# Second attention: GpSimd scales the exponentials, TensorE turns them with transposes, and two weight splits move into the loop of units

## The reference

```
s_loc = einsum(q, k_window) * scale + bias        # 384 columns in the kernel, masked with -1e30
s_ctx = einsum(q, k_ctx) * scale                  # 256 columns
p = softmax(concat([s_loc, s_ctx]), axis=-1)
o = einsum(p_loc, v_window) + einsum(p_ctx, v_ctx)
o = o * silu(c_z)                                 # later in the block
```

## Time and profile before

| | |
|---|---|
| median of 3 runs | 2630.74 us (2629.36 to 2631.32) |
| span of the profiled execution, first to last instruction | 2631.7 us |
| TensorE busy | 2435.6 us (93%) |
| VectorE busy | 1163.6 us (44%) |
| ScalarE busy | 854.4 us (32%) |
| GpSimd busy | 764.2 us (29%) |
| mean granted TensorE clock | 0.965 of full |
| second attention, first units to last | 1431 us to 1820 us of the span |

### The profile page before, as it was taken

The page is one execution under the profiler, slowest core; times in us unless marked ns, Lnnn a source line. Parts: engine busy times, 40 slices in busy tenths (PEclk is TensorE's granted clock), DMA queues, the critical chain, the costliest instruction groups (busy, mean ns, idle before and its releaser), DMA issues.

```text
span 2631.7 us, 32586 instructions
## 1 busy us (share of the span) xinstructions
PE 2435.6 (93%) x12094; PEld 2045.6 (78%) x12094; DVE 1163.6 (44%) x1376; ACT 854.4 (32%) x1137; POOL 764.2 (29%) x667
## 2 busy tenths in 40 slices
PE   2797999887999999999978989889999999999997
PEld 2686888776888888888767888879778888888885
DVE  7766888685442344234453351625221121222234
ACT  3225777314221122124444343434112111112221
POOL 3343222241333333333312111020223333333331
PEclk8897999998999999999988999999999999999998
DMA  5310000550111111111121101101001111111131
GB/s 222 137 66 34 25 16 25 216 208 32 48 48 48 48 48 48 48 58 50 38 95 59 61 27 50 52 16 62 32 28 48 48 48 52 48 48 40 48 120 72
DMA packets 45708, 165.49 MB, mean 63 GB/s; under 512 B 4048, under 2 KB 5840, under 8 KB 44496
## 3 DMA queue, kind: packets, MB, share of 16 engines
q1 hardware_dynamic: 45648, 164.67, 17.7%
HBM read 156.26 MB, written 8.39 MB: 63 GB/s over the span
## 4 chain that ended last, share of the span: by engine, by line
PE 83%; DVE 9%; ACT 4%; issue 2%; DMA 1%; POOL 0%; DVEq 0%; SPq 0%; ACTq 0%; POOLq 0%
PE acc L597 63%; PE bank L833 3%; PE turn L820 3%; PE turn L698 2%; PE bank L712 2%; DVE ADA L1290 2%; PE acc L681 2%; PE bank L698 1%; PE acc L806 1%; PE bank L588 1%; DVE K2L L1629 1%; DMA XT<-in_xT 1%; PE turn L615 1%; PE bank L876 1%; DVE K2L L1630 1%
## 5 line engine op out<-in xcount | busy, mean ns | idle before, releaser
L597 PE MATMUL acc<-HH,WH 128*128 128x512 f32 x1888 | 592.1, 395 | 50.5 <-POOL HL L508 29.5
L597 PE MATMUL acc<-HL,WH 128*128 128x512 f32 x1888 | 585.4, 391 | 0.0
L597 PE MATMUL acc<-HH,WL 128*128 128x512 f32 x1888 | 584.7, 391 | 0.0
L495 POOL TENSOR_TENSOR WH<-WF,CON 128x16 fp32r<-128x16 f32 x186 | 53.6, 288 | 1576.8 <-PE acc L597 1437.2
L597 PEld LDWEIGHTS acc<-HH,WH 128*128 128x128 f32 x1888 | 354.5, 189 | 134.3 <-POOL HL L508 25.9
L498 POOL TENSOR_TENSOR WL<-WF,WH 128x1024 fp32r<-128x1024 f32 (+2 forms) x186 | 439.4, 2362 | 15.5
L597 PEld LDWEIGHTS acc<-HL,WH 128*128 128x128 f32 x1888 | 357.7, 189 | 75.2
L597 PEld LDWEIGHTS acc<-HH,WL 128*128 128x128 f32 x1888 | 356.5, 189 | 75.0
L1542 DVE SCALAR_TENSOR_TENSOR CV<-EV,VEC,CV 128x1023 f32<-128x1023 f32 x44 | 105.5, 2397 | 242.4 <-ACT CV L1093 242.4
L1489 DVE TENSOR_TENSOR XT<-XT,EV 128x1024 f32 (+1 forms) x40 | 98.0, 2451 | 209.1 <-ACT EV L1074 209.1
L496 POOL TENSOR_SCALAR WH<-WF 128x1008 fp32r<-128x1008 f32 (+2 forms) x186 | 190.3, 1023 | 0.0
(11 more groups left out here) (293 smaller groups left out, 3701.5 us busy)
## 6 DMA issues: line engine op xcount, KB each, us to landing
WF<-in_w SPq DMA_DIRECT2D x150, 512.0 KB, 3.2
ADA<-in_ada SPq DMA_DIRECT2D x13, 2048.0 KB, 15.6
BIAS<-in_bias SPq DMA_DIRECT2D x8, 1152.0 KB, 5.1
ADA<-in_ada SPq DMA_DIRECT2D x6, 1024.0 KB, 4.9
WF<-in_w SPq DMA_DIRECT2D x24, 256.0 KB, 2.6
XT<-in_xT SPq DMA_DIRECT2D x2, 2048.0 KB, 13.0
ADA<-in_ada SPq DMA_DIRECT2D x8, 512.0 KB, 3.3
XT<-in_xT SPq DMA_DIRECT2D x8, 512.0 KB, 16.9
```

Of the source, the lines that this page charges most:

```text
L495: pool.tensor_tensor(h[:, 0:FEW], f[:, 0:FEW], zero.to_broadcast([P, FEW]), ALU.add).then_inc(w_hi, 1)
L597: last = pe.matmul(acc[:, slot, HALF * c:HALF * c + HALF], w[slot][:, k, :], x[:, k, HALF * c:HALF * c + HALF], start=(k == 0 and w is WH ...
```

## The change

In the second attention the diagonal is gone. VectorE only forms the reciprocal of the sum (`invert_sums`). GpSimd multiplies the exponentials in place by it (`normalise2`: a piece of 16 columns, then 624 columns), and signals `exn2_ready` twice. TensorE waits for both signals and turns each block by `pe.transpose` with the identity matrix in the constants. Since GpSimd now has an instruction pair in each unit, the loop of splits is cut up: the tiles of the pair's own gemms n+2 and n+3 are split ahead of its units, tile n+4 behind normalise2(2), tile n+5 behind normalise2(8). In the last pair these two are the first two tiles of the next stage (N_F and N_F + 1), so the loop behind starts at N_F + 2. The DG buffers remain in use in the first attention.

```diff
-            for n0, count, k1 in ((N_ATT2, 12, KD), (N_GF, 16, 4), (N_A, 8, KD), (N_GA, 8, 4), (N_OUT2, 4, KD)):
+            def normalise2(u0, u):
+
+                pool.wait_ge(rc_ready, u0 + (64 + u + 1))
+                x, r = EX2[u % 3], RC[:, u % 2:u % 2 + 1]
+                pool.tensor_tensor(x[:, 0:FEW], x[:, 0:FEW], r.to_broadcast([P, FEW]), ALU.mult).then_inc(exn2_ready, 1)
+                pool.tensor_scalar(x[:, FEW:], x[:, FEW:], r, None, ALU.mult).then_inc(exn2_ready, 1)
+
+            split_w(N_ATT2, 0, KD)
+            split_w(N_ATT2 + 1, 1, KD)
+            with pool.Fori(0, 4) as it:
+                n = it * 4 + N_ATT2
+                split_w(n + 2, 0, KD)
+                split_w(n + 3, 1, KD)
+                for u in range(16):
+                    normalise2(it * 16, u)
+                    if u == 2:
+                        split_w(n + 4, 0, KD)
+                    if u == 8:
+                        split_w(n + 5, 1, KD)
+            for n0, count, k1 in ((N_F + 2, 3, KD), (N_GF, 16, 4), (N_A, 8, KD), (N_GA, 8, 4), (N_OUT2, 4, KD)):
...
                 def turn_probs(u):
-                    pe.wait_ge(dg_ready, u0 + (u + 1))
+                    pe.wait_ge(exn2_ready, 2 * u0 + (2 * u + 2))
...
                         for k in ks:
-                            mm = pe.matmul(turn[:, part_col(k):part_col(k) + P], EX2[u % 3][:, P * k:P * k + P], DG[u % 2][:, :],
-                                           start=True, stop=True)
+                            mm = pe.transpose(turn[:, part_col(k):part_col(k) + P], EX2[u % 3][:, P * k:P * k + P], ident)
...
-                def diagonal(u):
+                def invert_sums(u):
                     dve.wait_ge(exp2_done, u0 + (u + 1))
                     dve.reciprocal(RC[:, u % 2:u % 2 + 1], SUM[:, u % 2:u % 2 + 1]).then_inc(rc_ready, 1)
-                    dve.wait_ge(rc_ready, u0 + (64 + u + 1))
-                    dve.tensor_scalar(DG[u % 2][:, :], ident, RC[:, u % 2:u % 2 + 1], None, ALU.mult).then_inc(dg_ready, 1)
```

More of the change, by code:

```diff
@@ L296, in build @@
         vt2_done, vtok2_ready = sem("vt2_done"), sem("vtok2_ready")
-        scores2_done, nb2_ready, exp2_done, dg_ready, pt2_done, pt2_ready, pv2_done, o2_ready = (
-            sem("scores2_done"), sem("nb2_ready"), sem("exp2_done"), sem("dg_ready"), sem("pt2_done"), sem("pt2_ready"),
+        scores2_done, nb2_ready, exp2_done, exn2_ready, pt2_done, pt2_ready, pv2_done, o2_ready = (
+            sem("scores2_done"), sem("nb2_ready"), sem("exp2_done"), sem("exn2_ready"), sem("pt2_done"), sem("pt2_ready"),
             sem("pv2_done"), sem("o2_ready"))
@@ L1634, in _ @@
                 for u in range(16):
-                    diagonal(u)
+                    invert_sums(u)
                     if u < 14:
```

## The result

The changed kernel takes 2648.4 us (median of 4 runs, 2643.98 to 2649.19), the kernel before 2631.0 (4 runs, 2629.36 to 2633.36). The forecast was 2598.5 us with a range up to 2620. The kernel got slower in the way of rival C (the scaling on GpSimd sets the pace), and on top of it the clock fell behind some of the stalls, as in rival A.

The account below looks back on a forecast made before the run. TensorE was taken to set the pace in the units. Per pair 2.9 + 7.7 - 3.8 + 1.3 = 8.1 us, times four 32, off 2631.7 less 1.0 gave 2598.5 us, range 2589 to 2620.

Parts of the forecast that it names:

- rival C: In the units, between reciprocal and turning: GpSimd's scaling sets the pace, at 2.3 us each, time 2639; chance 0.06.
- rival A: At 8 stalls TensorE's clock falls, one to two half-clock units each, 16 to 32 us, time about 2621; chance 0.17.
- step 3: GpSimd's 624-column scaling in each unit takes 0.71 us, 0.91 with the small piece, leaving 0.4 us of slack.
- Step 1: Start of a pair: with the split of tile n+5 gone, TensorE's wait for K2L shortens by 2.9 us.
- B: Start of a pair: GpSimd isn't what slows K2L, so moving the split gains nothing there; time 2610; chance 0.11.
- Step 2: Turning by transposes: five blocks take 0.56 us instead of 1.12, a steady unit 2.26; gain 7.7 us a pair.
- D: Turning: a block's transpose costs as much as the product did, 7.7 us less a pair, time 2633; chance 0.02.
- Step 4: Splits behind normalise2(2) and normalise2(8) each stall TensorE by 1.9 us, costing 3.8 us a pair.
- Step 5: Start of a pair, from first scores through the first turning and second unit, partly at half clock: gain 1.3 us.

Follow-up runs that it names:

- e3_wide: The changed kernel with one GpSimd tensor_tensor over all 640 columns as the scaling, in place of both instructions: 2617.31 us, ratio 0.9942 to the kernel before.
- e5_move_only: The kernel before, diagonal kept, with only the splits of tiles n+4 and n+5 held back to units 2 and 8: 2616.99 us, ratio 0.9944.
- e11_two_ops_pieces: The changed kernel with two-operation scaling, n+4's split ahead of the units and n+5's in six pieces behind scalings of units 2 to 7: 2590.1 us.
- e10_two_ops: The changed kernel with a second multiplication, by 1.0, added to the 624-column scaling: 2603.22 us, ratio 0.9891 to the kernel before.
- e8_ptr_ahead: The changed kernel with its slow scaling, but both splits (n+4, n+5) ahead of the units as before the change: 2627.28 us, ratio 0.9984.

## Why the prediction was wrong

**The step that failed is step 3**, the duration of the 624-column scaling. "0.60 + 128 x 0.83 ns = 0.71" was read from L496, a tensor_scalar on GpSimd of the same types. The group's row names operation, tiles and shape, but not how many arithmetic operations the instruction holds. L496 in the code is `1.0, 1.0, ALU.mult, ALU.mult`, the new line `r, None, ALU.mult`. The difference is to be seen in the two lines and isn't in any row. With the two-operation form the instruction takes 0.785; with the one written, 1.843. The upper end of 2.3 us held it, but for a wrong reason (contention), and so with too small a chance: rival C had 0.06. C's own formula with 2.05 us for a scaling gives 6 x 0.75 + 3 x 1.14 = 7.9 us a pair, a time of 2630; C left out that the slack is gone before each stall, and the fall of the clock behind some of them; measured were 2648.

With the right duration the working of step 3 gives what is measured. Scaled exponentials of u + 2 are ready 4.12 - 0.91 + 2.05 = 5.26 us behind turning u (L575's 0.21 and L576's 1.84). In the second pair, after, two units take 2.35 + 2.91 = 5.26. With e3_wide's 1.255 in one instruction it gives 4.47, under two units of 2.29, and the units there aren't lengthened. In the second half of each pair two slow units take 5.5 instead of 5.26; why, I didn't trace.

**Step 1 was right.** L1646 takes 0.42 each time and the wait is 2.87 in all four pairs, as forecast; B falls. Alone it is worth 14 us (e5_move_only), 2.6 more than 4 x 2.87. Of these, 1.1 lie in the units: the first turning starts 4.50 us behind the first scores instead of 5.07, and the unit behind it gives half of that back. The rest is open. The Trainium skill (GPSIMD Engine Reference, Specifications) says that GpSimd's SBUF interfaces are shared with VectorE, with contention where VectorE has two SBUF inputs or a two-port mode; K2L's 0.42 against 2.56 us agrees with the first.

**Step 2 was nearly right.** Turning starts and next scores are 0.47 us apart instead of 1.03, the 0.56 forecast. The unit is 2.29 to 2.35 instead of 2.26, because the values' matmuls now take 1.31 to 1.35 instead of 1.28, with short waits for ScalarE's copies. The last distances went from 2.63 to 2.29, the 0.34 forecast. D falls. Between e5_move_only and e11_two_ops_pieces, which differ by the way of turning and scaling and by where the splits stand, lie 27 us. The units alone are 31.2 us shorter in the profiled executions, of which 29, or 7.2 a pair, lie behind the second turning's start, against the 7.7 forecast; the projections, with their clock, take back the difference.

**Step 4 was right for the scaling it assumed.** It said that turning 3 starts 4.16 us after turning 2; e10_two_ops has 4.12 to 4.13 (4.00 to 4.13 at the second stall). With the slow form there is no slack left to absorb any of it: split 3.65 and scaling 2.05 make 5.7, measured 5.5 to 5.6. The pieces of e11_two_ops_pieces take the stalls away altogether. They win 15.5 us in the units of the profiled executions, where the prediction had priced the eight stalls at 8 x 1.9 = 15, and 13 us in the medians.

**Step 5 was too good.** Of 1.3 us a pair, e10_two_ops shows 0.4, 0.5, 1.1 and 0.7 in the four pairs, 0.7 in the mean: from first scores to second turning 9.4, 9.6, 9.7 and 9.9 us before, 9.0, 9.1, 8.7 and 9.1 in e10_two_ops. The first turning runs at half clock in all pairs of both.

**Rival A** took part. Waits of 1.5 to 1.7 us left the clock at 2.4 GHz in 8 of 8 cases (e10_two_ops). Behind waits of 2.1 to 2.3 us it fell in 3 of 8 (e3_wide), behind waits of 3.0 to 3.1 us in 5 of 8 (the changed kernel), and a unit then takes 3.8 to 4.3 us instead of 2.3 to 2.4. A had priced 8 to 16 such units; there are 5. Why not behind the other three stays open. The Trainium skill (TensorE: Matmul & The Clock Gate, PE-mode transpose) says that transposes don't count as activity. No run here tests it: in e11_two_ops_pieces every unit has five of them in 2.29 us and the clock stays whole, but products fill the rest of the unit; where the values are turned, with transposes and waits, it was 1.00 in one pair and 0.50 in the next.

**The sum.** e10_two_ops against the forecast, 2603.2 against 2598.5, is the net error of all the other steps, 4.7 us, in which the clock of the projections has a part. The form costs the remaining 45.2. Of the changed kernel's 58.3 us over e11_two_ops_pieces, 25.7 are the slow units and starts (2627.3 - 2590.1 less the 11.5 of K2L's extra wait in e8_ptr_ahead) and the remaining 32.6 the eight stalls with their falls of the clock. This split takes the parts as additive, which no single run shows.

## What to carry to other kernels

When a new instruction is priced from a row of the profile, lay the two source lines beside each other: operation name, shape and types in the row can agree and the form still differ by a factor of 2.6. Where an engine off the path is put on it, read from the rows how long it idles between two of its deadlines (here 1.3 us) and keep every other job on it shorter than that, in pieces if need be. Pieces cost more in sum than the whole: four quarters took 2.9 us where the one instruction took 2.35. And a forecast whose sign hangs on one borrowed duration should give its rival the chance that the duration is wrong, not only the chance that neighbours slow it.

## What the hardware showed that I had not expected

GpSimd's tensor_scalar on 128x624 fp32 in place takes 1.843 us with one operation and a factor from SBUF, 1.770 with one and a constant, 0.785 with two operations of which one reads the factor, 0.712 with two constants. Why a second operation makes it faster, no run tells. The Trainium skill (GPSIMD Engine Reference, Elementwise side by side) has about 1.8 cycles an element for a tight loop, 0.94 us for 624 columns as an estimate; none of the four is there, two are quicker and two about twice as slow. A tensor_tensor of 640 columns with the factor broadcast lies between, at 1.252 us.

VectorE's tensor_scalar with a single SBUF tensor, 0.55 us, takes 2.23 beside GpSimd's tensor_tensor of 2.36 us. So it isn't only instructions with two SBUF tensors that suffer from a split. The other condition that the Trainium skill (GPSIMD Engine Reference, Specifications) names, a two-port mode of VectorE, may be met here; no run shows the mode.
